# A fused hybrid layer: input blocks summed on VectorE, squares of x read again later, and two chunks of v beside the turning of x

## The reference, cut to what matters

```
xn   = rms_norm(h, g_pre_mix)
proj = xn @ w_in            # columns: q | k | v | gate_b | gate_c | conv_in, 1024 each
attn = stick-breaking attention(q, k, v)          # 8 heads
conv = gate_b * short_conv(gate_c * conv_in)      # 8 groups of 128 channels
mix  = concat(rms_norm per head of attn, rms_norm per group of conv)
h   += rms_norm(mix @ w_out)
h   += rms_norm(swiglu(rms_norm(h)))
```

## Time and profile before

| | |
|---|---|
| time, 3 runs | median 2391.86 us (2391.11 to 2392.72) |
| profiled execution | 2392.84 us, span 2391.1 us, mean granted TensorE clock 0.995 |
| PE busy | 2349.9 us (98%) |
| DVE, ACT, POOL busy | 1704.0 (71%), 1114.0 (47%), 93.8 (4%) |
| DMA | 366.23 MB, 153 GB/s |

### The profile page before, as it was taken

The page is one execution under the profiler, slowest core; times in us unless marked ns, Lnnn a source line. Parts: engine busy times, 40 slices in busy tenths (PEclk is TensorE's granted clock), DMA queues, the critical chain, the costliest instruction groups (busy, mean ns, idle before and its releaser), DMA issues.

```text
span 2391.1 us, 42660 instructions
## 1 busy us (share of the span) xinstructions
PE 2349.9 (98%) x18156; PEld 2311.7 (97%) x18156; DVE 1704.0 (71%) x1964; ACT 1114.0 (47%) x1412; POOL 93.8 (4%) x158
## 2 busy tenths in 40 slices
PE   7899999999999999999999999999999999999999
PEld 6899999999998999999999999999999999999998
DVE  4766644444445568877787877877777788888887
ACT  6544335555555455444444444444444433333346
POOL 0100000000002110000000000000000000000002
PEclk9999999999999999999999999999999999999999
DMA  8344343323325875245444344543535775654562
GB/s 280 113 135 130 115 134 93 93 82 112 102 74 157 238 205 177 92 137 163 139 155 148 129 155 138 169 142 128 162 125 172 268 249 199 225 190 126 178 209 89
DMA packets 377008, 366.23 MB, mean 153 GB/s; under 512 B 9548, under 2 KB 330468, under 8 KB 376308
## 3 DMA queue, kind: packets, MB, share of 16 engines
q1 hardware_dynamic: 341200, 295.63, 39.9%
q10 hardware_dynamic: 35620, 67.89, 7.9%
HBM read 295.60 MB, written 67.88 MB: 152 GB/s over the span
## 4 chain that ended last, share of the span: by engine, by line
PE 89%; DVE 3%; DMA 3%; ACT 2%; issue 2%; SPq 1%; POOL 0%; ACTq 0%; DVEq 0%; POOLq 0%
PE ps L1206 37%; PE ps L1265 18%; PE ps L549 12%; PE ps L1040 8%; PE ps L1100 7%; PE ps L903 4%; PE ps L847 1%; DMA w_raw<-in_w_in_dram 1%; DMA ff_lo_scr<-hid_lo 1%; PE ps L1173 1%; DMA w_raw<-in_w_out_dram 1%; ACT w_hi L529 0%; DVE w_lo L535 0%; PE ps L1155 0%; SPq L698 0%
## 5 line engine op out<-in xcount | busy, mean ns | idle before, releaser
L1206 PE MATMUL ps<-xs,t_hi 128*128 128x272 f32 x4832 | 915.7, 289 | 4.0 <-ACT m L1713 4.0
L1206 PEld LDWEIGHTS ps<-xs,t_hi 128*128 128x128 f32 x4832 | 759.0, 188 | 4.4 <-issue 4.0
L1206 PE MATMUL ps<-xs,t_lo 128*128 128x272 f32 x2416 | 697.2, 289 | 0.0
L2232 DVE TENSOR_TENSOR t_lo<-panel,t_hi 128x1024 fp32r<-128x1024 f32 (+1 forms) x400 | 479.7, 1199 | 217.6 <-ACT t_hi L1680 214.5
L1680 ACT CAST t_hi<-panel 128x1024 fp32r<-128x1024 f32 (+1 forms) x400 | 408.1, 1020 | 432.3 <-PE ps L1265 234.1
L1265 PE MATMUL ps<-xd,t_hi 128*128 128x272 f32 x2464 | 466.8, 289 | 3.0 <-DVE y_left L2407 1.1
L1206 PEld LDWEIGHTS ps<-xs,t_lo 128*128 128x128 f32 x2416 | 455.5, 189 | 0.0
L1265 PEld LDWEIGHTS ps<-xd,t_hi 128*128 128x128 f32 x2464 | 386.9, 188 | 4.4 <-issue 4.4
L1265 PE MATMUL ps<-xd,t_lo 128*128 128x272 f32 x1232 | 355.6, 289 | 0.0
L1265 PEld LDWEIGHTS ps<-xd,t_lo 128*128 128x128 f32 x1232 | 231.7, 188 | 0.0
L535 DVE TENSOR_TENSOR w_lo<-w_raw,w_hi 128x1024 fp32r<-128x1024 f32 x92 | 114.8, 1249 | 161.5 <-ACT w_hi L529 161.5
(11 more groups left out here) (247 smaller groups left out, 3293.0 us busy)
## 6 DMA issues: line engine op xcount, KB each, us to landing
panel<-in_w_up_dram SPq DMA_DIRECT2D x44, 1024.0 KB, 5.2
panel<-in_w_gate_dram SPq DMA_DIRECT2D x43, 1024.0 KB, 5.0
panel<-in_w_down_dram SPq DMA_DIRECT2D x32, 1024.0 KB, 6.3
w_raw<-in_w_in_dram SPq DMA_DIRECT2D x56, 512.0 KB, 4.1
ff_hi_scr<-hid_hi SPq DMA_DIRECT2D x22, 952.0 KB, 4.5
ff_lo_scr<-hid_lo SPq DMA_DIRECT2D x22, 952.0 KB, 7.4
in_raw<-in_w_in_dram SPq DMA_DIRECT2D x40, 512.0 KB, 4.0
w_raw<-in_w_out_dram SPq DMA_DIRECT2D x36, 512.0 KB, 4.6
```

The lines of the kernel that those rows point to most:

```text
L1206: mm = nc.tensor.matmul(out, w[:, k, :], xs[x][:, part, k, :], start=begins and k == 0 and w is hi and part == 0, stop=k == KH - 1 and w i ...
L2232: V.tensor_tensor(tile_of(t_lo, i), raw_tile(i), tile_of(t_hi, i).bitcast(F32), ALU.subtract)\
```

## The change

It has seven parts.

1. All 16 turned chunks have a place of their own (12 in `misc`, 4 in `h_more`), so no copy waits for a store. Turned chunks use two pairs of PSUM banks, not three.
2. Beside the turning TensorE multiplies two chunks of v (`acc[0]` and `acc[1]`), six matmuls each per turned chunk; tiles 0 to 3 are chunk 0 and 1, first halves, then second halves. All eight front tiles are loaded to the four places of `in_raw`; tiles 0 and 1 ahead of the second part of x, tiles 2 and 3 behind the third part.
3. The quarters of the input are not loaded from DRAM and not scaled: VectorE adds `act_hi` and `act_lo` (`in_block`), and makes all sums and rests; GpSimd does nothing there.
4. x is not squared in the turning. It is loaded once more in 20 pieces of 512 columns (`load_x_again`, 24 transfers to one buffer) in the steps of seven products, and ScalarE squares three pieces a step (`square_x`). The sums (`diagonals`, `input_sums`, `make_rstd(0)`) come at the end of step 7.
5. `load_in_tile` of step 0 waits for the rests of tiles 4 to 7 one by one.
6. Behind the steps VectorE makes the first rest of the next weights ahead of the copy of the cache's keys.
7. At the output projection VectorE does `conv` of the last group ahead of `mix_head` of the last head, and `last_norm_and_rows` stands behind c = 10, not c = 6.

```diff
@@ places and banks
-        RING = 8
-        h_ring = misc[:, D:end].rearrange("p (s t) -> p s t", s=RING)
+        H_NEAR = 12
+        h_near = misc[:, D:end].rearrange("p (s t) -> p s t", s=H_NEAR)
+        h_more = sb_at("h_more", 120832, [P, KC - H_NEAR, T])
-            return ps[:, 2 + 2 * (c % 3) + j // 3, (j % 3) * P:(j % 3) * P + n]
+            return ps[:, 4 + 2 * (c % 2) + j // 3, (j % 3) * P:(j % 3) * P + n]
@@ SyncE
             load_x(0)
             load_first(0)
+            load_first(1)
             load_x(1)
             load_x(2)
-            load_first(1)
+            for k in range(2, 4):
+                load_first(k)
...
             for j in range(IN_STEPS):
-                for b in ((IN_B12, IN_B11, IN_B21, IN_B22) if j else (IN_B11, IN_B12, IN_B21, IN_B22)):
+                for m, b in enumerate((IN_B12, IN_B11, IN_B21, IN_B22) if j else (IN_B11, IN_B12, IN_B21, IN_B22)):
                     load_in_tile(j, b)
+                    if j and m < 3 and 3 * (j - 1) + m < SQUARES:
+                        load_x_again(3 * (j - 1) + m)
+            def load_x_again(k):
+                part, j = k // (QB + 1), k % (QB + 1)
+                f = slice(part * XQ_N, (part + 1) * XQ_N)
+                if k:
+                    sp.wait_ge(x_squared, k)
...
+                elif j < QB:
+                    sp.dma_start(x_again[:, :], xp[j * P - NMETA:(j + 1) * P - NMETA, f]).then_inc(x_reloaded, 16)
@@ TensorE
-            front_chunk(1, [input_sums] + [lambda: None] * 3)
             for c in range(2, FRONT):
                 front_chunk(c, [lambda: None] * 4)
             for j in range(IN_STEPS):
+                if j == SUMS_STEP + 1:
+                    input_sums()
...
-                if c == 6:
+                if c == 10:
                     last_norm_and_rows()
@@ VectorE
+            def in_block(out, c0, t):
+                tokens = slice(t * HALF, (t + 1) * HALF)
+                hi, lo = (act[:, c0:c0 + KH, tokens].bitcast(F32) for act in (act_hi, act_lo))
+                V.tensor_tensor(out[:, :, :], hi, lo, ALU.add).then_inc(in_s_made, 1)
...
+            rest_of_weights((PAIR_T, 0, FRONT_T), 0)
             dve.wait_ge(kc_turned, 1)
...
+            conv(GROUPS - 1)
             mix_head(HEADS - 1)
-            conv(GROUPS - 1)
@@ ScalarE, in each of the steps 0 to 6
                 in_copy(j, T2, "a", 1, 0)
+                if 3 * j < SQUARES:
+                    square_x(3 * j)
                 in_tile_high(7 * j + B22)
                 in_copy(j, T3, "b", 1, 1)
+                if 3 * j + 1 < SQUARES:
+                    square_x(3 * j + 1)
@@ GpSimd
-            for k in range(1, LEAD):
-                rest_of_weights((FRONT_T, 0, 0), k, nc.gpsimd)
-            G.tensor_tensor(in_s_raw[S3][:, :, :], in_s_raw[S2][:, :, :], in_s_raw[S1][:, :, :], ALU.subtract)
-            G.tensor_tensor(in_s[S3][:, 1, :, :], in_s_raw[S3][:, :, :], in_s[S3][:, 0, :, :].bitcast(F32),
```

More of the change, by code:

```diff
@@ L287, in build_layer @@
         diag_ready = sem("diag_ready")
-        h_stored = [sem(f"h_stored{j}") for j in range(RING)]
+        h_stored = sem("h_stored")
+        x_reloaded = sem("x_reloaded")
         sq_made = sem("sq_made")
@@ L304, in build_layer @@
         in_stored = [sem(f"in_stored{j}") for j in range(2)]
-        a_loaded = [sem(f"a_loaded{j}") for j in range(2)]
-        in_s_scaled = sem("in_s_scaled")
         in_s_made = sem("in_s_made")
-        in_s3_made = sem("in_s3_made")
+        in_s_hi = sem("in_s_hi")
+        in_s_lo = sem("in_s_lo")
         hi_ready = sem("hi_ready")
@@ L427, in tile_used @@
             per, r, first = phase
+            if per == FRONT_T and k < 4:
+                return (first_used, chunk_done)[k // 2], k % 2 + 1
             sem_of = (first_used, chunk_done)[k % 2]
@@ L462, in raw_slot @@
         def raw_slot(phase, k):
+            if phase[0] == FRONT_T:
+                return in_raw[:, k % 4, :]
             if out_tile(phase, k) == 4 * KC + 5:
@@ L476, in raw_loaded, with in_arrived, x_reloads @@
                     return out_loaded[k % 2], 16 * in_place
-                return w_loaded[k % 2], 16 * (loads_of((4, WIDER // 4, T_OUT), k % 2 - 2) + in_place)
-            return w_loaded[k % 2], 16 * loads_of(phase, k)
+                return w_loaded[k % 2], 16 * (loads_of((4, WIDER // 4, T_OUT), k % 2 - 2) - FRONT_T // 2 + in_place)
+            if phase[0] == FRONT_T:
+                return in_loaded[k % 4], 16 * (k // 4 + 1)
+            return w_loaded[k % 2], 16 * (loads_of(phase, k) - FRONT_T // 2)
+        def in_arrived(j, b):
+            return in_loaded[b], 16 * (FRONT_T // 4 + j + 1)
+        SUMS_STEP = (SQUARES + 2) // 3
+        assert SUMS_STEP + 1 < IN_STEPS
+        def x_reloads(k):
+            j = k % (QB + 1)
+            return 16 * (sum(2 if i % (QB + 1) in (0, QB) else 1 for i in range(k + 1)))
         def last_in_slot(slot):
@@ L586, in panel_of @@
         def panel_of(step, half):
-            before = 16 * IN_STEPS
+            before = 16 * (FRONT_T // 4 + IN_STEPS)
             if step == 0:
@@ L676, in load @@
                     sp.wait_ge(norm_summed, HEADS + GROUPS)
-                elif not known(t) or t >= 2:
+                elif t < FRONT_T:
+                    if t >= 4:
+                        sp.wait_ge(lo_ready, t - 3)
+                else:
                     sp.wait_ge(lo_ready, t - 1)
@@ L756, in _ @@
             sp.wait_ge(v_stored, 48 * HEADS)
-            for j in range(RING):
-                sp.wait_ge(h_stored[j], 16 * (KC // RING))
+            sp.wait_ge(h_stored, 16 * KC)
             for q in range(2, KC):
@@ L1946, in _ @@
             V.memset(eps[:, :], EPS)
+            V.memset(sq_acc, 0.0)
             V.memset(sq_sums[:, :, :], 0.0).then_inc(const_ready, 1)
@@ L2067, in _ @@
                 in_add(j, T4, "b", 1, 0)
+                if j == SUMS_STEP:
+                    diagonals()
                 if more:
```

225 lines of the change are left out of this document (101 added, 124 removed).

## The result

The changed kernel takes 2397.66 us (median of 8 runs, 2396.76 to 2402.86) against 2392.52 us before: ratio 1.0026, interval [1.0017, 1.0035]. The forecast was 2386.9 us, so it is on the other side of no change, and outside the range.

The account below looks back on a forecast made before the run. TensorE was taken as the bound, busy 98% of the span, so only its waits and low clock could be won. Terms -6.1 + 1.4 - 1.2 + 1.0 = -4.9 from 2392.84, less 1.0 to the median: 2386.9 us; range 2381 to 2393.

Parts of the forecast that it names:

- A, the turning: Start: turned chunks of 2.37 us from the sixth at 19.9; TensorE done with two v chunks at 50.6.
- Rival 2: Turning slower than its matmuls, by late bank copies or crowded transfers: 0.3 us per cycle, 2390 us; chance 0.14.
- A, from there on: Start behind the turning: copy_front waits of 7.8 and 2.5 us, two clock falls, step 0 ends at 110.8: -6.1 us.
- E, the reload: Steps of seven products: squares and 3.0 us landings of re-read x hidden in 3.3 us of room: 0.
- rival 3: Late reload: ScalarE waits for x_again, rounding queued behind, TensorE waits for those weights: 14 us lost, 2400.9; chance 0.07.
- the signs of being wrong: ScalarE waits at squares, then TensorE's for w_hi or w_lo; block additions over 3 us; turned chunk over 2.5.
- B: Sums of x leave the start and stand ahead of step 8: 1.51 us of TensorE, net +1.4.
- C: Behind the steps: first rest ahead of the cache keys' copy, TensorE starts at about 312.2: -1.2 us.
- D: Output projection: the 4.86 us wait moves behind the sums; waits about 1.5, 1.0 and 4: +1.0, -0.7 without clock fall.
- the second fall: Start: clock falls again behind chunk 3's wait of 2.5 us, costing 1.8; without it the start gains 7.9.
- the split that the text describes: Likeliest case half each side of 0.2%, clock case beyond, turning and half of in_block within: faster 0.50, same 0.41.

Follow-up runs that it names:

- e2: Changed kernel with a second place for the re-read pieces of x, so a piece may be fetched one square earlier: 2394.26 us, ratio 1.0005 to the kernel before.
- e3: Changed kernel, still one place for the pieces of x, each next piece fetched by ScalarE's own queue behind its square: 2399.87 us, ratio 1.0028 to the kernel before.
- e6: Changed kernel with weight tiles 2 and 3 rounded two turned chunks earlier and two places for the pieces of x: 2390.34 us, ratio 0.9991 to the kernel before.
- e8: e7 with tiles 4 to 7 loaded among the stores, 4 and 5 split in the turning, copy_front earlier and in_s rests reordered: 2382.28 us, ratio 0.9957.
- e10: e7 with only tiles 4 to 7 loaded among the stores and 4 and 5 split in the turning; VectorE's order stays: 2383.47 us, ratio 0.9964.
- e7: e6 with part 7 undone (mix_head ahead of conv, last_norm_and_rows behind c = 6): 2386.75 us, ratio 0.9979 to the kernel before.
- e11: e8 with the four copy_front copies out of PSUM made by ScalarE, not VectorE: 2377.47 us, ratio 0.9940 to the kernel before.

## Why the prediction was wrong, point by point

- **A, the turning: the step that failed.** "I take the sixth turning to start at about 19.9", "the sixteenth then starts at 19.9 + 10 x 2.37": that sum took the weights of k = 8 to 15 to be ready. They were not, by the position of one rounding in ScalarE's order: 2.28 us of wait and about 3.1 at 1.2 GHz (granted clock 0.50). With the 1.0 us of the later start, most of which other executions don't show, this is 6.4 of the 6.6 us between 50.6 and 57.15. Cycles of 2.37 us were right (18.48, 20.86, 23.24). Rival 2 said that the turning might be slower than its matmuls, but by the banks or by late transfers; neither showed: the cycles are as forecast, and the wait for the first part of x was 3.16 us in this execution, 1.9 to 2.8 in the nine others with the new start and 2.25 before.
- **A, from there on: right.** 8.29 and 1.96 us of wait against 7.8 and 2.5, the clock at 0.50 behind both, additions of blocks at 2.49 us, no operation of 7.24 us. Step 0 ended 7.4 late, of which 6.6 came in with the turning.
- **E, the reload: the second step that failed,** by the room more than by the landing. "the second square would start behind the rounding, at 194.59 + 1.04 = 195.7": that rounding is of the next step's weights, and the square stands ahead of it, behind the copy of T3, which ended at 194.28 + 0.41 = 194.7 in the trace before. So the room was 194.7 - 192.4 = 2.3 us, not 3.3, and even the forecast's landing of 3.0 us would not have been hidden from ScalarE. Measured were 1.8 to 2.3 us of room and 3.8 of landing (256 KB, 3.0 to 5.3), so ScalarE waits up to 2.0 us a step. The mechanism is the first half of rival 3, which had a chance of 0.07: ScalarE waits with the rounding queued behind it. TensorE then waited not for the weights, as rival 3 and the signs of being wrong had it, but for VectorE's addition of T1 at B22. Not all squares reach TensorE, so seven steps lose 4.1 us in the trace, not 14; by the ratio e2 gives back 5.0.
- **The rule of the Trainium skill** ("DMA: Bandwidth & Descriptors", section "Anatomy of one DMA") gave an estimate of 2.6 us; its fit is for GpSimd's path, and these transfers are SyncE's and, in e3, ScalarE's. The trace disagrees here: 256 KB beside a weight tile took 3.3 to 4.5 in the median (e3, the changed kernel, e2), and the weight tile itself went from 4.0 to 4.6 in that stretch.
- **B, C, D: right.** +1.2 against +1.4; -1.25 against -1.2; +1.7 against +1.0, with waits of 1.71, 0.80 and 3.69 where 1.5, 1.0 and about 4 stood.
- **The sum.** -4.9 + 7.4 (A) + 4.1 (E) + 0.7 (D) - 0.2 (B) = +7.1, the ledger's figure. e6, which takes both unforeseen losses out and leaves the rest of the change as it is, has the ratio 0.9991, 2.2 us below the kernel before; its interval reaches to 0.9982, 4.3 below, and the forecast stood at 4.9 with D sized 0.7 too low. That is close, and what may be left was not followed. Two figures beside the sum don't follow from its terms: without the second fall and with D at -0.7 the terms give 2383.4, not 2381; and by the split that the text describes, the chances come to 0.45 for faster and 0.46 for the same, not 0.50 and 0.41.
- **Where more of the start's gain lay.** That the wait for `copy_front` is in large part the place where TensorE waits for VectorE's list, and would wait later if the copies came sooner, was in no step of the forecast. In e8, with the copies moved, TensorE waits 2.94 at B22 and the chain up to it is VectorE's. Taking 2.3 + 1.2 us of work and waiting off that list (e10 against e7) gave 3.3 us by the times, 3.6 by the ratios and 2.2 at B22 in the traces; moving the copies besides (e8 against e10) gave 1.2, 1.7 and 3.6, the first two within the noise; taking 2.6 us more off the list, and ScalarE's late copy (e11 against e8), gave 4.8, 4.1 and 4.3. Both the list and the place of the copies count, and their shares are not settled.

## What to carry to other kernels

When work is put beside other work, read for each operand the place of its maker in the maker's own order, not only the engine's free time: here one rounding two chunks too late cost 5.4 us in the trace, more than the 4.9 that the whole change was to bring, with the engine idle beside it. A transfer into a single buffer, issued only when its reader is done, has its whole landing on that reader's engine: count its room up to the first place where the new order reads it, take the slowest landing of the nearest rows for it, or give it a second place. And before a wait is moved, ask what the engine that is waited for has to do up to the next meeting point: where its list is the bound, moving the wait gives less than its length (from e7 to e8 8.8 us of wait for `copy_front` went, and B22 came 5.8 sooner), and work taken off the list counts.

## What the hardware showed that was not expected

- A 256 KB piece with one other stream beside it lands in 3.0 to 5.3 us in one execution (2.8 to 3.9 in e3, 3.7 to 6.0 in e2); a median says little on whether a given slack is enough.
- Whether the granted clock falls behind a wait isn't told by its length alone. Behind 1.96 us (changed kernel, row above) it stood at 0.50; behind 1.81 us (e6) and 1.74 us it stayed at 1.00. But at the start of the output projection it stayed at 1.00 in the changed kernel behind waits of 1.71 and 0.80 us, and in e2 it fell behind the same two waits, there 1.69 and 0.79. The window of e6 behind its wait at 76.42, of the changed kernel behind 739.44, and of e2 behind 734.34:

```profile
76.42:82.42 6.00, 6.00 (x46) 6.00 (x47) 5.75 (x4) 1.68 (x2) 0.00 (x0) 1.00 0.44 155
```

```profile
739.50:742.90 3.40, 3.40 (x27) 3.32 (x28) 2.53 (x7) 3.23 (x9) 0.00 (x0) 1.00 0.55 154
```

```profile
734.20:737.40 3.20, 3.06 (x13) 3.10 (x14) 2.73 (x7) 3.11 (x7) 0.00 (x0) 0.50 0.60 164
```
